# Feed-forward entry: a unit's low half behind the entering tiles, high-part products first, products with ones in the waits

## The reference, cut to what matters

```python
mixed = jnp.concatenate([oa, ob, oc], axis=-1) @ w_out[l]
h = h + rms_norm(mixed, norm_mix_post[l])                       # residual
f = causal_dwconv(rms_norm(h, norm_ffn_pre[l]) @ ffn_up[l], ffn_conv[l])
gate, val = jnp.split(f, 2, axis=-1)
f = (jax.nn.gelu(gate, approximate=True) * val) @ ffn_down[l]
h = h + rms_norm(f, norm_ffn_post[l])
```

## Time and profile before

| | |
|---|---|
| median of 3 runs | 945.93 us (945.59 to 949.43) |
| the profiled execution | 948.21 us |
| its span, first to last instruction | 946.5 us |
| mean granted clock of PE | 0.994 |
| busy, share of the span | PE 98%, PEld 91%, DVE 73%, ACT 55%, POOL 24% |
| DMA | 150.21 MB, 159 GB/s mean |
| chain that ended last, by engine | PE 92%, DVE 3%, ACT 2%, issue 2%, POOL 1% |

### The profile page before, as it was taken

How to read it: one execution, slowest core, us unless ns; L and a number is a source line. 1 busy time by engine, 2 the same in 40 slices (tenths; PEclk the granted TensorE clock), 3 DMA queues, 4 the chain that set the end, 5 groups by cost and what they waited for, 6 DMA issues and landing times.

```text
span 946.5 us, 19686 instructions
## 1 busy us (share of the span) xinstructions
PE 925.4 (98%) x7966; PEld 862.3 (91%) x7966; DVE 691.4 (73%) x1063; ACT 520.6 (55%) x941; POOL 225.8 (24%) x194
## 2 busy tenths in 40 slices
PE   8999999989999999999999999999899999999997
PEld 7999888979999988789999899998699998999995
DVE  6988875477999895567878675576659787655684
ACT  8653465456556664564665565544646565554443
POOL 3445221430221221004223130042033132300140
PEclk9999999989999999999999999999999999999999
DMA  8543200236555555456534535555284444545551
GB/s 318 179 157 112 75 20 2 78 101 199 181 178 184 182 180 189 159 206 247 175 125 144 172 124 192 181 187 192 83 307 156 157 157 133 168 159 188 182 176 45
DMA packets 41562, 150.21 MB, mean 159 GB/s; under 512 B 4608, under 2 KB 4864, under 8 KB 41216
## 3 DMA queue, kind: packets, MB, share of 16 engines
q1 hardware_dynamic: 39456, 141.54, 44.8%
q10 hardware_dynamic: 2016, 7.41, 2.2%
HBM read 147.88 MB, written 1.05 MB: 157 GB/s over the span
## 4 chain that ended last, share of the span: by engine, by line
PE 92%; DVE 3%; ACT 2%; issue 2%; POOL 1%; DMA 0%; DVEq 0%; SPq 0%; ACTq 0%; POOLq 0%
PE ps L728 89%; PE ps L1063 2%; ACT whi L1280 1%; DVE wlo L1696 1%; PE ps L1169 1%; ACT xh L1280 0%; DMA raw<-in_ws 0%; DVE S L1696 0%; ACT tmp L1280 0%; ACT L1280 0%; POOL ocf L2276 0%; DVE ht L1704 0%; DVE pcraw L1696 0%; POOL fS L2276 0%; DVE rr L1738 0%
## 5 line engine op out<-in xcount | busy, mean ns | idle before, releaser
L1280 ACT ACTIVATE whi<-raw 128x1024 fp32r<-128x1024 f32 (+1 forms) x264 | 278.1, 1055 | 297.2 <-PE ps L728 289.5
L728 PE MATMUL ps<-xh,whi 128*128 128x256 f32 (+2 forms) x1440 | 413.7, 287 | 4.0 <-DVE wlo L1696 1.4
L1696 DVE TENSOR_TENSOR wlo<-raw,whi 128x1024 fp32r<-128x1024 f32 (+1 forms) x256 | 324.0, 1269 | 119.9 <-ACT whi L1280 119.0
L728 PE MATMUL ps<-xl,whi 128*128 128x256 f32 (+2 forms) x1440 | 408.2, 283 | 1.6 <-DVE xl L1704 1.6
L728 PE MATMUL ps<-xh,wlo 128*128 128x256 f32 (+2 forms) x1440 | 407.4, 283 | 0.0
L728 PEld LDWEIGHTS ps<-xh,whi 128*128 128x128 f32 x1440 | 272.1, 189 | 10.6 <-issue 8.6
L728 PEld LDWEIGHTS ps<-xl,whi 128*128 128x128 f32 x1440 | 271.5, 189 | 2.8 <-DVE xl L1704 2.2
L728 PEld LDWEIGHTS ps<-xh,wlo 128*128 128x128 f32 x1440 | 272.5, 189 | 0.0
L2276 POOL TENSOR_TENSOR gts<-gts 128x256 f32<-128x256 f32 x32 | 30.2, 955 | 150.5 <-DVE gts L1704 149.9
L728 PE MATMUL ps<-yh,whi 128*128 128x256 f32 x232 | 65.3, 281 | 0.0
L728 PE MATMUL ps<-yl,whi 128*128 128x256 f32 x232 | 65.2, 281 | 0.0
(11 more groups left out here) (345 smaller groups left out, 1327.8 us busy)
## 6 DMA issues: line engine op xcount, KB each, us to landing
raw<-in_ws SPq DMA_DIRECT2D x262, 512.0 KB, 3.4
h<-in_rel ACTq DMA_DIRECT2D x2, 1024.0 KB, 13.5
qc<-in_gam ACTq DMA_DIRECT2D x3, 512.0 KB, 5.2
mt<-in_m ACTq DMA_DIRECT2D x2, 576.0 KB, 6.1
h<-in_hT SPq DMA_DIRECT2D x4, 272.0 KB, 5.5
gts<-in_lng ACTq DMA_DIRECT2D x2, 512.0 KB, 8.3
out<-ht SPq DMA_DIRECT2D x4, 256.0 KB, 2.0
gts<-in_g ACTq DMA_DIRECT2D x2, 448.0 KB, 10.3
```

The source lines that it names most:

```text
L728: return e.matmul(o, l, r, start=start, stop=stop, skip_group_check=True)
L1280: return e.activation(o, a, f, bias=bias, scale=scale, accum_out=acc)
L1696: return e.tensor_tensor(o, a, b, op)
```

## The change

Three things, all in the feed-forward's entry. (1) In DVE's order the low half of the entry's fourth unit moves from between residual 0 and xl 0 to behind xl 6; and the reciprocal at the end of the entry comes ahead of the fourth low half (that of the seventh unit) rather than behind it. (2) For stage 1, PE takes a tile k in another order: for each of the three output tiles hi x xh and lo x xh, and only then, behind one wait for xl, the three products hi x xl. (3) Products of ones with ones: the pulse of stage 1 has 17 rather than 14, and between the products with xh and those with xl stand 3 more for k = 0, 2 for k = 1 and 1 for k = 2 (`beat` 8 to 10). They go into the bank that the next tile would be given (`next_of`), without taking it. DVE's order becomes: residual 0, xl 0, residuals 1 and 3, xl 1, residual 4, xl 2, xl 3, residuals 6 and 7, xl 4, 5 and 6, low half of the fourth unit, xl 7, two low halves, the reciprocal, a low half, evacuations. The orders of PE's steps, ACT, POOL and SP are the same.

```diff
-BEATS = (3, 1, 1, 2, 1, 1, 4, 4)
+BEATS = (3, 1, 1, 2, 1, 1, 4, 4, 3, 2, 1)
...
+    def next_of(self, banks):
+        b = banks[self.turn[banks] % len(banks)]
+        return b, self.holder.get(b)
...
         "dve": (
-            "hwdhhhhdhddhhddwddwwdddwddwcdwcdwvcwdcdwvcwdcwdvcdwcwdvcwdcwdvwcdwcdwvcdwcwdvcwdcwdvcwdcwdvwcdwcdw"
+            "hdhhhhdhddhhdddwdwwdwddwddwcdwcdwvcwdcdwvcwdcwdvcdwcwdvcwdcwdvwcdwcdwvcdwcwdvcwdcwdvcwdcwdvwcdwcdw"
...
+            def next_bank(banks):
+                b, before = book.next_of(banks)
+                if before is not None and not book.counting:
+                    pe.wait_ge(*book.freed_by[before])
+                return tiles[b]
...
                 if k in (2, 4, 6):
                     squares(st, k - 1)
+                if st:
+                    enter_turned(st, k)
+                    return
...
+            def enter_turned(st, k):
+
+                n, parts = NT[st], []
+                pe.wait_ge(("x.hi", st, k))
+                for key in first_keys(st):
+                    hi, lo, said = take()
+                    o = ps_of(key)[:, 0:n]
+                    mm(o, hi, xh[:, k, 0:n], k == 0, False)
+                    mm(o, lo, xh[:, k, 0:n], False, False)
+                    parts.append((o, hi, ([("tile", key)] if k == 7 else []) + said))
+                if k < 3:
+                    beat(8 + k)
+                pe.wait_ge(("x.lo", st, k))
+                for o, hi, said in parts:
+                    t = mm(o, hi, xl[:, k, 0:n], False, k == 7)
+                    if said:
+                        t.then_inc(*pe.says(*said))
...
             def pulse(st):
...
-                for i in range(14):
+                for i in range(17 if st else 14):
                     t = mm(ps[:, 0:128], ones, ones, True, True)
...
             def beat(i):

-                ps = bank(PJ0, ("beat", i))
+                ps = bank(PJ0, ("beat", i)) if i < 8 else next_bank(PJ1)
                 pe.wait_ge(("c.ones",))
                 for _ in range(BEATS[i]):
                     t = mm(ps[:, 0:128], ones, ones, True, True)
-                t.then_inc(*pe.says(("beat.d", i), frees=("beat", i)))
+                t.then_inc(*pe.says(("beat.d", i), frees=("beat", i) if i < 8 else None))
```

## The result

| | before | after |
|---|---|---|
| median | 946.31 us (944.57 to 949.52, 15 runs) | 944.99 us (943.25 to 948.47, 15 runs) |
| profiled execution | 948.21 us, span 946.5 | 943.49 us, span 941.7 |
| mean granted clock in it | 0.994 | 0.999 |
| ratio | | 0.9977, 95% interval 0.9967 to 0.9988 |

The change makes the kernel 0.23% faster, some 2.2 us by the ratio; the two medians of the table are 1.3 us apart. Two more comparisons of the same kernel gave ratios of 0.998 (0.997 to 0.9989) and 0.9979 (0.9966 to 0.9992).

What follows compares the result with a forecast made beforehand. The prediction took PE, idling and losing its clock in the feed-forward's entry, to bound the kernel. For the median run 1.0 (low half) + 2.4 (clock) - 0.7 (ones) = 2.7 us, from 945.93 to 943.2 us, range 941.0 to 946.4.

Steps and rivals of the forecast that it cites:

- What bounds it: Feed-forward entry: PE loses to idle gaps and a halved clock; a microsecond saved before 217 is one of the end.
- Part 1: DVE at the entry: moving the low half starts the transposes at about 203.6 and gains 1.0 us, bounds 0.6 and 1.5.
- Part 2: PE's entering tiles: high-part products first only keep PE busy; the transposes start no earlier, so no time is gained.
- Part 3: PE's entry: ones in the pulse and tile 0 hide in waits; those of tiles 1 and 2 cost 0.7 us.
- Part 4: PE's entry: the clock holds; 6.1/2 = 3.0 us returns in the profile, 2.4 for the median run.
- lower bound of 1.7: Clock term of the entry: least gain, taken from a short low stretch of 3.4 us like layer 1's.
- Rival (a): Entry: the clock falls all the same, with the last gap and the transposes; 0.8 us slower, 946.7; chance 0.14.
- The signs asked for: Entry: clock 1.00, first product still about 200.5, transposes about 203.6, next tile about 213.9, no wait for the low half.
- Rival (b): Layer entries: the clock's loss there changes, 1.7 us each, giving 941.5 or 944.9; forecast with this luck has chance 0.74.
- (c): End of the entry: the moved low half, or xl behind it, is late; 1.7 us come back, 944.9; chance 0.05.
- (d): Entry: it gains more than its parts, some earlier runs having lost more than the profile; 940.5 to 941.2; chance 0.05.
- (e): Whole kernel: over 0.5% slower, needing 4.7 us; nearest cause a late unit load in the steady stage; chance 0.02.

Runs made afterwards that it cites:

- low_half_only: The kernel before with only DVE's order of the change (low half moved, reciprocal swapped); mean 945.41 us, ratio 0.999 to before.
- no_ones: The change without any of its new products with ones, so high-part-first order and moved low half only; mean 944.79 us, ratio 0.9983 to before.
- order_only: The kernel before with only PE's high-part-first order, without the moved low half or new ones; mean 948.13 us, ratio 1.0014 to before.
- first_ones: The change without the ones behind tiles 1 and 2, compared twice (again as first_ones_2); mean 944.54 us, ratios 0.9972 and 0.9987 to before.
- eight_ones: The change without the ones behind tiles 1 and 2, and eight products with ones behind tile 0 instead of three; mean 944.72 us, ratio 0.9973 to before.
- layer_ones_2: The change without ones behind tiles 1 and 2, plus three at the entries of layers 0 and 1; mean 943.72 us, ratio 0.9974 to before.
- before_x2: The kernel before, unchanged, profiled a second time; its feed-forward entry took 15.35 us, and the kernel's mean over 89 executions is 946.52 us.

## Why the prediction held, step by step

**What bounds it** was right: PE alone behind 205, every us of the entry a us of the end. The output tile after the entry starts 3.24 us earlier in the profile (216.98 - 213.74), the transposes that open layer 0 3.26 earlier (398.66 and 395.40), and with the 1.5 us of layer 1 that is the 4.7 us of the span.

**Part 1, the moved low half**, forecast 1.0: the transposes come 3.10 us behind the first product, from 4.14, so 1.04. low_half_only gives 0.98 by itself, and order_and_ones, which has everything of the change but the moved low half, has its transposes 4.08 behind. POOL went otherwise than I had it: its product took 0.73 and not up to 1.71, with xl beside it at 0.99, so DVE paid and POOL didn't. A rule of the Trainium skill ("SBUF — State Buffer", section "Who interferes with whom") had who pays right: POOL started first, at 200.18, and ran unhindered; xl, from 200.21, took 0.99 where it takes 0.48 alone. The smaller gain of 0.6 that I had worked out by it did not come, since xl had paid the same before (0.95). The rows before also say by which order the two wait, which I had denied: POOL's h of 0.79 us from 199.58 ran in its usual time, the low half from 199.71 took 1.75 where it takes 1.23 later, and POOL's product from 200.34, begun inside the low half, is the one of 1.71. The low half ran at 209.5 and nothing waited for it; the swapped reciprocal cost nothing either.

**Part 2, the order**, forecast as nothing in time. That was wrong, though small. Behind the transposes low_half_only, at full clock, takes 10.24 us to the last square (205.25 to 215.49), no_ones 9.64 (204.99 to 214.63). The two differ only in the order of the products: 0.6 us, nearly all of it at tile 2. The old order wants xl after one product and sits through a late one with the rest of the tile undone; the new one does six products first. I had written that xl of tiles 2 and 3 is there before PE. In the new order it is (no wait there in no_ones), in the old one, at full clock, it is not, and that is what I had put at nothing. The 0.6 rests on two profiles: order_only, which fell, gained nothing, and of the executions at a mean clock of 0.997 low_half_only has a median of 944.7 and no_ones of 944.6.

**Part 3, the ones.** The pulse and the three behind tile 0 are hidden, as forecast. The three behind tiles 1 and 2 cost 0.4 and not 0.7, since without them some 0.24 us are lost at tile 4, whose xl is late (2.85 - 2.61). The step that failed is the same as in part 2: I held DVE's xl to be early throughout. What the ones are good for may show only where the low half is not moved: order_and_ones has a mean of 946.36 and 4 of 12 that kept the clock, order_only 948.13 and none, though not in the same comparison. Beside the moved low half, no_ones and the change have the same mean.

**Part 4, the clock.** The direction was right. In all eight profiles of kernels that have both the low half moved and the order turned (the change three times, first_ones twice, eight_ones, no_ones, layer_ones_2) the entry kept its clock; the kernel before lost it in three of three. With the whole change, and without its last three ones, it held wherever the first product came: at 200.4, 201.7 and, in first_ones, 203.6. Which part holds it, the runs leave open. Of the 14 profiles the nine with the low half moved kept the clock in the entry, low_half_only with PE's order of before among them, and the five without lost it, order_and_ones too; so the moved low half is the simplest reading. But 4 of 12 executions of order_and_ones kept the clock throughout, and low_half_only and no_ones reached the entry 1.5 us late, behind a low stretch further up. Idle time does not tell the cases apart. The gaps of order_and_ones, which fell, were 0.52, 0.21 and 1.61, those of low_half_only and no_ones, which did not, 1.13, 0.57 and 1.00, and 1.19 and 1.62; and in the 5 us from 1.5 ahead of the first product PE was busy for 3.24 in the first, for 2.29 and 2.19 in the others. Rival (a) did not come. I had given it a reason by the Trainium skill ("TensorE: Matmul & The Clock Gate", "Part 4: PE-mode transpose"); no run separates the transposes from the wait ahead of them, but filling that wait changed nothing.

The size was wrong. With the other terms measured, the profile's 3.14 us of the entry split into: 1.04 for the low half, 0.60 for the order, -0.38 for the ones, and as the remainder 1.88 for the clock, where I had 3.0. That remainder is the difference between two profiles with the same order of products: 12.12 us from the transposes to the last square before (204.62 to 216.74), 10.24 in low_half_only. The step that failed is "6.1/2 = 3.0": it took PE's half-rate work as wholly regained. Part of it covered waits for xl that a full clock brings out, 0.56 and 0.31 us at tiles 2 and 4 in low_half_only (3.17 and 2.92 against 2.61). In before_x2 the same working gives 15.35 - 13.12 = 2.23 and leaves 1.0 for the clock. My lower bound of 1.7 was too high; with one short stretch it must be less still: 31 of the 89 executions before had a mean clock of 0.997 (3 thousandths of 944 us at half clock are 5.7, of which 2 to 3 lie at the kernel's end, so one stretch of 3.4), and their median of 945.5 stands 1.9 over the change's 943.6, of which 1.04 + 0.60 - 0.38 = 1.26 are the other terms, so 0.6 for the clock. That is worked out, not measured by a profile, and each comparison by itself gives less: 945.5 against 944.4 in the one and 945.2 against 943.6 in the other, and so -0.2 and 0.4.

**The number.** Forecast 2.7 us and 943.2; measured 2.2 by the ratio, 1.8 by the means of all executions, 1.3 by the medians, the change's being 944.99. The signs asked for came: the first product at 200.38, the transposes at 203.48, the tile after the entry at 213.74. In the profile the parts were forecast to give 3.3, and the transposes of layer 0 start 3.26 earlier; that near hit is luck, since its terms were wrong both ways. Of the difference to 943.2, 0.4 is the kernel before, which came out at 946.31 in 15 runs and not at 945.93, and the rest is what two errors of opposite sign left over: the clock too dear by 0.5 to 1.8 us, the order and the ones together too cheap by 0.9. Rival (b), the luck of the layers' entries (and of the mixer and the first ten us, which I had not counted), is most of what spreads the runs: 18 of 38 executions of the change lost a stretch somewhere, at 1.5 us. I had counted it as a shift and not as the usual case: a median of 943.6 is what the executions without a loss have, and just over half are such. Rivals (c), (d) and (e) have left no trace.

## What to carry to other kernels

Where PE waits in short gaps for several engines, look for what lies on the chain but isn't wanted yet, and put it behind them; a moved instruction gave its 1.0 us as read off the chain. Neither the longest gap nor the sum of the gaps foretold here whether the clock holds. Let PE first do everything that doesn't need the operand that comes last: between two profiles at full clock it was worth 0.6 us, and by itself (order_only) nothing. When a low clock goes away, don't take half of the slow work as the gain: run the order of arrivals again at the full clock, and see which input is late next. And where times stand in steps, compare the steps (here by the mean clock of each execution) before the medians, and only between executions of one comparison.

## What the runs showed of the hardware

The same code lost its clock in one execution and kept it in another: in the first ten us and at layers 0 and 1 (the three profiles of the change), in the mixer from 152.9 (first_ones, not first_ones_2), and in or ahead of the feed-forward's entry (order_and_ones: lost at 205.4 in its profile, kept throughout in 4 of 12). The low stretches of the 14 profiles were 3.4 or 6.8 us long, but for the one that reaches the end.

The clock also falls where PE is busy by the profile. In order_only's mixer (stages: length, busy us of PE, PEld, DVE, ACT, POOL, clock):

```profile
149.00:152.00 3.00, 3.00 (x42) 2.42 (x40) 2.26 (x8) 1.06 (x4) 0.76 (x1) 1.00 0.00 0
152.00:156.00 4.00, 4.00 (x24) 2.21 (x24) 1.75 (x5) 1.70 (x8) 1.15 (x1) 0.58 0.00 0
```

PE's busy time there is 3.00 of 3 us and then 4.00 of 4, and the clock fell at 152.6 all the same, for 6.8 us. Many of the products there are small, with weights of 64 x 64, 16 x 64 and 2 x 128 beside the full ones (PE's groups by form, 149 to 153):

```profile
L732 PE MATMUL ps<-LRb 2*128 2x144 f32 x8 | 0.8, 307 | 0.0
L732 PE MATMUL ps<-fPT,vk 16*64 16x16 f32 x8 | 0.4, 209 | 0.0
```

Their size by itself doesn't decide it. The kernel before has the same code there and was as busy, and in its profile the clock stayed at 1.00:

```profile
152.00:156.00 4.00, 4.00 (x49) 2.66 (x51) 2.52 (x8) 1.84 (x9) 1.10 (x1) 1.00 0.00 0
```

It is the place at which low_half_only and first_ones lost their clock too (from 155.0 and 152.9). What is left to gain there, by an estimate from the 1.5 us that a short low stretch costs 1.5 to 3 us in such an execution, was not tried.
